# Cross attention's keys and values moved from their own stage into the core of the causal attention

## The reference: what is computed

```
x = x + memory_cross_attention(rmsnorm_2(x, norm_xa_w), rmsnorm_2(mem, norm_mem_w), wq, wkv, wo)

def memory_cross_attention(h, m, wq, wkv, wo):
    q = (h @ wq).reshape(b, s, XA_HEADS, XA_HEAD_DIM)
    k, v = jnp.split(m @ wkv, 2, axis=-1)
    scores = einsum('bshd,bmhd->bhsm', q, k) * XA_HEAD_DIM ** -0.5
    o = einsum('bhsm,bmhd->bshd', softmax(scores), v)
    return o @ wo
```

## Time and profile before

| | us |
|---|---|
| median of 3 runs | 2833.64 |
| lowest and highest | 2833.48, 2842.4 |
| the profiled execution's own time | 2844.55 |
| its span, from the first to the last instruction | 2842.8 |
| mean granted clock of PE | 0.949 |
| PE, DVE, POOL, ACT busy, share of the span | 84%, 57%, 52%, 24% |

### The profile page before, as it was taken

How to read it: one execution, slowest core, us unless ns; L and a number is a source line. 1 busy time by engine, 2 the same in 40 slices (tenths; PEclk the granted TensorE clock), 3 DMA queues, 4 the chain that set the end, 5 groups by cost and what they waited for, 6 DMA issues and landing times. The chain is left out here.

```text
span 2842.8 us, 28049 instructions
## 1 busy us (share of the span) xinstructions
PE 2389.1 (84%) x9104; PEld 1549.9 (55%) x9104; DVE 1634.2 (57%) x3467; ACT 690.4 (24%) x1777; POOL 1476.5 (52%) x962
## 2 busy tenths in 40 slices
PE   7999679998989988889886888888877777777776
PEld 6888567786878848767564344444322322222222
DVE  1266695224532648640228788888778777555555
ACT  2111234123421230222322222222222222111112
POOL 6777345673267712276365565666544444333432
PEclk9999789999899978889998999999999999999999
DMA  3222001221022200022226999999999999999996
GB/s 130 96 96 96 1 1 52 89 87 48 32 77 94 96 8 1 8 80 98 74 96 277 419 421 421 420 413 411 419 422 421 422 421 421 422 421 422 421 422 265
DMA packets 103878, 642.63 MB, mean 226 GB/s; under 512 B 12624, under 2 KB 13008, under 8 KB 38096
## 3 DMA queue, kind: packets, MB, share of 16 engines
q0 software_dynamic: 73728, 536.90, 45.5%
q1 hardware_dynamic: 30032, 104.24, 11.0%
HBM read 639.00 MB, written 2.10 MB: 226 GB/s over the span
## 5 line engine op out<-in xcount | busy, mean ns | idle before, releaser
L3041 PE MATMUL bank<-peer_row,peer_diag 128*128 128x512 f32 x2048 | 961.5, 615 | 284.8 <-ACT peer_diag L3020 283.8
L2963 POOL DMA_INDIRECT peer_row<-in_peer_uv,peer_ids x512 | 581.4, 1136 | 658.0 <-PE bank L3041 612.8
L3041 PEld LDWEIGHTS bank<-peer_row,peer_diag 128*128 128x128 f32 x2048 | 377.2, 193 | 838.3 <-ACT peer_diag L3020 451.6
L2986 DVE CUSTOM_DVE_ANT_0 peer_row<-peer_row,peer_h_tok 128x1024 f32<-128x1024 f32 x512 | 639.1, 1252 | 326.7 <-DMA peer_row<-in_peer_uv,peer_ids 326.6
L206 POOL TENSOR_TENSOR w_parts<-ring,zero 128x1024 fp32r<-128x1024 f32 x152 | 288.1, 1895 | 291.6 <-PE bank L283 129.4
L209 POOL TENSOR_TENSOR w_parts<-ring,w_parts 128x1024 fp32r<-128x1024 f32 x152 | 368.6, 2425 | 27.1 <-POOL w_parts L206 27.1
L3020 ACT ACTIVATE peer_diag<-ident,peer_weight 128x128 f32<-128x128 f32 x512 | 177.5, 394 | 241.5 <-DVE peer_weight L2978 241.5
L3024 ACT ACTIVATE peer_acts<-peer_dots 128x2 f32<-128x2 f32 x256 | 52.2, 204 | 743.3 <-DVE peer_dots L2986 743.3
L259 PE MATMUL bank<-ssm_h_high,w_parts 128*128 128x512 f32 x512 | 158.0, 389 | 0.8 <-DVEq L642 0.8
L259 PEld LDWEIGHTS bank<-ssm_h_high,w_parts 128*128 128x128 f32 x512 | 96.1, 188 | 21.0 <-DVEq L642 1.0
L2738 PE MATMUL bank<-peer_h_high,w_parts 128*128 128x512 f32 x256 | 107.4, 469 | 0.0
(11 more groups left out here) (542 smaller groups left out, 3841.8 us busy)
## 6 DMA issues: line engine op xcount, KB each, us to landing
ring<-in_weights SPq DMA_DIRECT2D x180, 512.0 KB, 3.3
peer_row<-in_peer_uv,peer_ids POOLq DMA_INDIRECT x512, 24.3
resid<-in_x SPq DMA_DIRECT2D x1, 2048.0 KB, 7.5
out<-resid SPq DMA_DIRECT2D x4, 512.0 KB, 7.6
xa_mem<-in_mem SPq DMA_DIRECT2D x1, 1024.0 KB, 4.9
peer_gain<-in_rows SPq DMA_DIRECT2D x2, 512.0 KB, 6.7
peer_keys<-in_peer_keys SPq DMA_DIRECT2D x1, 1024.0 KB, 7.3
ssm_o_gain<-in_rows SPq DMA_DIRECT2D x1, 512.0 KB, 3.4
```

The costliest lines, as they stand in the source:

```text
L2963: pool.indirect_dma_start(self.rows[row][:, :], None, self.m.ins["peer_uv"], bass.IndirectOffsetOnAxis(ap=self.choice.ids[:, t, slot:slot ...
L2986: dot = dve.tensor_tensor_reduce(mine, mine, self.tokens(slot_of(j)[0]), 1.0, 0.0, ALU.mult, ALU.add, self.dots[:, h % 4, r:r + 1])
L3041: mm = pe.matmul(self.m.banks[2 * t + half][:, :], self.diag[:, j % (2 * GROUP), :], self.rows[row][:, D + half * 512:D + (half + 1) * 512 ...
```

## The change

The normalised memory and the products with the weights of keys and values leave `hybrid_out_cross_in`:

- `mamba_out_attention_in` now also loads and normalises the memory. ACT issues the load after the norm that it has just made, waits for it, and then goes on; DVE sums squares and makes the diagonals ahead of the rotary angles; PE transposes the memory in two halves between units of the last chunk of the projection.
- `attention_core` gets 16 weight units: 8 for the values and 8 for the keys, both by `column`. One column stands before the first unit's turn, the others at the end of each unit. They share bank 7, so all of the attention's values go to bank 6, and values(u) waits for DVE's unit u-1. ACT copies each column out. The values come out with channels in the partitions; after units 4, 5, 8 and 9 PE turns four tiles of them (float32 transposes) and ACT copies these too. POOL splits the 16 units itself, both parts. SP stores values and keys (1 MB each) to a tensor in DRAM, and waits for the stores before the block's barrier.
- `hybrid_out_cross_in` is left with the mixer's output and the queries. At the end of its weight stream SP loads values and keys from DRAM and waits for them before the barrier. `high_weight` and `low_weights` are gone.
- In DRAM the weight units of keys and values stand behind the attention's input weights.

```diff
 def attention_core(...):
+        side = m.banks[7]
+        turn_after = {4: (0, 0), 5: (0, 1), 8: (1, 0), 9: (1, 1)}
+        copies_before = lambda u: u + sum(n < u for n in turn_after)
...
         @block.sync
             sp.dma_start(sinks[:, :], m.row("att_sinks", QH)).then_inc(sink_loaded, 16)
+            stream_weights(m, sp, N)
+            sp.wait_ge(side_copied, copies_before(max(turn_after)) + 2)
+            sp.dma_start(m.kept[0], mem_v[...]).then_inc(side_stored, 16)
+            sp.wait_ge(side_copied, N + len(turn_after))
+            sp.dma_start(m.kept[1], mem_k[...]).then_inc(side_stored, 16)
+            sp.wait_ge(side_stored, 32)
...
         @block.gpsimd
+            split_weights(m, pool, N)
...
         @block.tensor
             def values(u):
-                if u >= 2:
-                    pe.wait_ge(out_ready, u - 1)
+                if u >= 1:
+                    pe.wait_ge(out_ready, u)
...
+            def side_column(u):
+                pe.wait_ge(m.w_split, u_side + u + 1)
+                if u >= 1:
+                    pe.wait_ge(side_copied, copies_before(u))
+                column(m, pe, u, mem_h, side[:, 0:MEM]).then_inc(m.w_used, 1)
...
             scores(0)
             scores(1)
+            side_column(0)
             for u in range(N):
                 turn(u)
                 if u + 2 < N:
                     scores(u + 2)
+                if u in turn_after:
+                    side_turn(u)
                 if u >= 1:
                     values(u - 1)
+                if u + 1 < N:
+                    side_column(u + 1)
             values(N - 1)
...
         @block.scalar
                 if u >= 1:
                     turned_copy(u - 1)
+                act.wait_ge(m.w_used, u_side + u + 1)
+                to = values_ch[:, u, :] if u < DT else mem_k[:, u - DT, :]
+                act.activation(to, side[:, 0:MEM], ACT.Copy).then_inc(side_copied, 1)
...
 def hybrid_out_cross_in(...):
         @block.sync
-            sp.dma_start(mem[:, :, :], ins["mem"].rearrange("(t p) d -> p t d", p=P)).then_inc(mem_loaded, 16)
-            stream_weights(m, sp, 2 * DT + 2 * DT)
+            stream_weights(m, sp, 2 * DT)
+            sp.dma_start(v_tok[...], m.kept[0]).then_inc(kept_loaded, 16)
+            sp.dma_start(k_ch[...], m.kept[1]).then_inc(kept_loaded, 16)
+            sp.wait_ge(kept_loaded, 32)
...
         @block.tensor
-                if ch == 0 and kk == 2:
-                    norm_m.tensor(pe)
...
-            columns_out(m, pe, DT, mem_h, MEM, k_copied, 1, m.banks[4:8])
-            pe.wait_ge(q_copied, DT)
-            tokens_out(m, pe, 2, DT, mem_h, MT, v_done, nothing, lambda ch, t: m.banks[MT * ch + t])
```

More of the change, by code:

```diff
@@ L120, in __init__ @@
         self.floor = nc.sbuf_base
+        self.kept = nc.dram_tensor("xa_kept", [2, P, MT * D], F32, kind="Internal").ap()
     def sem(self, scope, name):
@@ L215, in split_weights @@
         four(i, u0, False)
[L218 to L232, removed]
 PASSES = ((0, 0), (0, 1), (1, 0))
@@ L1200, in before_bank, with memory, scalar @@
                 pe.wait_ge(self.read, TT * (ch - 2) + t + 1)
-        tokens_out(self.m, pe, self.CH, DT, self.h, TT, self.done, before_bank, self.bank_of, self.h_ready)
-    def scalar(self, act):
+        def memory(ch, kk):
+            if ch == self.CH - 1 and kk in (1, 2):
+                pe.wait_ge(self.read, TT * (self.CH - 1))
+                norm_m.tensor(pe, range(4 * kk - 4, 4 * kk))
+        tokens_out(self.m, pe, self.CH, DT, self.h, TT, self.done, before_bank, self.bank_of, self.h_ready, memory)
+    def scalar(self, act, norm_m):
         qk, v, gate = self.qk, self.v, self.gate
@@ L1340, in values @@
                     for half in halves:
-                        mm = pe.matmul(m.banks[6 + u % 2][:, q * AD:(q + 1) * AD],
+                        mm = pe.matmul(m.banks[6][:, q * AD:(q + 1) * AD],
                                        pt[:, u % 2, q, half * P:(half + 1) * P],
@@ L1345, in values, with side_turn @@
                 mm.then_inc(pv_done, 1)
+            def side_column(u):
[3 more added lines that the diff above has]
+                column(m, pe, u, mem_h, side[:, 0:MEM]).then_inc(m.w_used, 1)
+            def side_turn(u):
+                half, t = turn_after[u]
+                pe.wait_ge(side_copied, copies_before(u) + 1)
+                for k in range(4):
+                    mm = pe.transpose(side[:, k * P:(k + 1) * P], values_ch[:, 4 * half + k, t * P:(t + 1) * P], m.ident[:, :])
+                mm.then_inc(side_turned, 1)
             for j in range(NT):
@@ L2352, in _ @@
             turn.tensor(pe)
-            def beside(ch, kk):
-                if ch == 0 and kk == 2:
-                    norm_m.tensor(pe)
-            def before_bank(ch, t):
-                if ch == 1 and t == 0:
-                    pe.wait_ge(norm_m.turned_ready, DT)
-            out.tensor(pe, before_bank, beside)
+            out.tensor(pe)
             for k in range(DT):
@@ L3142, in program @@
         set_up(m)
-        qk, v, gate = mamba(m)
-        attention(m, qk, v, gate)
+        mem_h = [m.at(8 + 8 * x, f"xa_mem_h_{y}", [P, DT, MEM], F32R) for x, y in enumerate(("high", "low"))]
+        qk, v, gate = mamba(m, mem_h)
+        attention(m, qk, v, gate, mem_h)
         q_ch, k_ch, v_tok, rms = hybrid(m, qk, gate)
```

96 lines of the change are left out of this document (47 added, 49 removed).

## The result

| | before | after |
|---|---|---|
| median (us) | 2833.95 (5 runs) | 2818.65 (5 runs) |
| lowest and highest | 2833.48, 2842.4 | 2814.88, 2819.56 |
| the profiled execution's own time | 2844.55 | 2814.88 |
| its span | 2842.8 | 2813.2 |

The ratio is 0.9935, with a 95% interval of 0.9919 to 0.9951: 15.3 us faster, where 27 were forecast. The time lies in the stretched range of 2799 to 2823, but 5.7 us above the forecast's own, 2800 to 2813. Between the two profiled executions, by which the sum was made, the difference is 29.7, against -27.3 in the sum (and -29.6 by the two spans). So two questions remain: whether each term holds, and where the other 12 to 14 us are.

What follows compares the result with a forecast made beforehand. Outside PEER's gathers, PE's work, idle time and half clock were taken to set the core and tail. Terms -58.1 + 0 + 27.3 + 1 - 1 + 1.5 + 2 = -27.3 gave 2807 us at the median; own range 2800 to 2813, stretched 2799 to 2823.

Steps and rivals of the forecast that it cites:

- Rival 1: Causal core: the clock falls as it does now, 18 us at half clock costing 9 instead of 2: 2814; chance 0.19.
- Rival 3: Core: DVE and POOL stand in each other's way; if all waited, 11 us more, 2818; chance 0.06.
- Rival 4: Stored tensors late: store 9 us more, loads up to 29 more; with a third of that 2820; chance 0.09.
- The tail, -58.1: Block ahead of the cross core: without key and value work the cross core starts at 1326.9 instead of 1385.04, -58.1 us.
- the transposes, 0: Memory's transposes leave one PE-bound block, -3.7 us, and enter another, +3.7: zero in sum.
- ACT's delay in the projection: Projection block: ACT waits for the memory, some 12 us, hidden by 16.99 us of idle time; bounds 0 to +3.
- The core, +27.3 + 1 + 2 = 30.3: Causal core: columns +27.3 us, keys' store at its end +1, short clock falls in its first units +2.
- No falls at all: Core: by the skill's clock rule, columns in every gap would prevent clock falls, a time about 2 us lower.
- The start of the cross core, +1.5: Cross core: PE's pause before it brings half clock in its 16 first matmuls, +1.5 of at most +3.7 us.
- The -1 for the transposes behind the core: Next block's first 32 transposes (5.81 us at half clock) could take 3.7 if PE stays busy: -1 of -2.1 us.
- Rivals 2: Half clock through most of the core; at three quarters of the core 2880 us; chance 0.08.
- the difference is carried over to the median: Whole kernel: the profiled execution's 10.9 us above the median was taken off 2817.3, giving 2806.3.

Runs made afterwards that it cites:

- early: Changed kernel with the loads of stored values and keys issued ahead of the weight stream instead of behind it: 2813.52 us, ratio 0.9926.
- slim: Changed kernel with POOL splitting the first four units whole and only 16 of 1024 columns of the other twelve, all 24 matmuls kept: 2818.07 us, ratio 0.9931.
- thin: Changed kernel with one matmul a column instead of 24; loads, splits, waits and copies kept: 2799.92 us, ratio 0.9883.
- first repetition: Kernel before, unchanged, profiled again the first time: profiled execution 2834.35 us, core 76.94 us.
- a_again: Changed kernel run and profiled once more, nothing edited: median 2817.29 us, ratio 0.9928.
- b_again: Kernel before, unchanged, the first of its three repeated profiles: profiled execution 2834.35 us; median of all repetitions 2834.1 us.
- The filled gaps: Changed kernel without columns in the core, plus 50 matmuls nobody reads before and behind the first turns: median 2781.9 us, 2780.66 in the second profile.

## Why the prediction came out as it did

The direction, the mechanism and, to about 1 us each, the terms made from rows of the first profile were right; the step to the median was wrong. The median's place in the range of 2799 to 2823 is luck: it is above the forecast's own 2800 to 2813, and what stretched the range to 2823, rivals 1, 3 and 4, did not come.

- **The tail, -58.1, and the transposes, 0.** By the block lengths the tail lost 61.9 with the transposes in it and their new block won 4.1: -57.8 in all. The loads ended last, as said. PE's pause is 3.63 us, 4.3 were in the sum (1322.6 to 1326.9); from start to start, the cross core begins 4.02 us behind the last query matmul, where 4 to 5 were given. Rival 4's third of late transfers did not come; the keys' store landed in 3.9 us and was hidden, so its +1 was 0.
- **ACT's delay in the projection** was hidden: PE's only visible change there is the transposes, 2 x 1.95 = 3.9 us, and ACT still idles for 10.40 us ahead of chunk 1, where the earlier trace rows have 16.99.
- **The core, +27.3 + 1 + 2 = 30.3** (columns, store, clock dips) against 30.4 measured in the first pair of profiles. That the two agree to 0.1 is in part luck, since the store's +1 was 0: up to DVE's last instruction the core grew from 82.8 to 113.0 us, 30.2 where 29.3 were given. The unit was 6.79 for 6.75. The clock fell twice, in the opening transposes (6.22 us for 4.56) and under the last values (2.66 for 1.90), 2.4 us for the 2 given. No falls at all, the prediction's other possibility, came true where columns stand and not at the core's two ends.
- **The start of the cross core, +1.5** was +1.7, and early shows it to be the pause's price. The -1 for the transposes behind the core was hardly there: 5.58 us against 5.81.
- **Rival 1** had the stretches of 694 to 718 right and their owner wrong. The falls are not what the change keeps, but what only the old core has, in changing amounts. **Rivals 2 and 3** did not come: no window of the steady core is under 1.00, and slim shows that POOL's splits in twelve of the units cost nothing. **Rival 3** names a real effect, though, which thin brings out once PE no longer covers it.
- **The step that failed**: "the difference is carried over to the median", by which 2817.3 became 2806.3, with 2818.65 measured. It took the 10.9 us between the profiled execution and the median as common to both kernels. The first repetition's span is 10.2 shorter than that profile's, 6.8 of it in the core itself (76.94 against 83.76), 2.2 ahead of the Mamba output and 1.2 behind the core. So some 7 us lay in the very stretch that the change rebuilds and fills, and the full core, at 1.00 in its steady part in each of its profiles, has no such fall to lose or to save. Against the typical core the columns cost 114.14 - 76.94 = 37.2, not 30.4; with the tail (162.68 us in that repetition too) and the projection block that makes -61.9 + 4.3 + 37.2 = -20.4 against the first repetition; the whole difference from that one to the profile after is 2814.88 - 2834.35 = -19.5. The medians, -15.3 and -17.8 in the two comparisons, are smaller by a few us, and the profile after was itself the fastest of its five. The other pair of profiles near the medians, a_again against b_again, has -61.7 + 4.1 + 38.0 = -19.6 in the three blocks and +4.6 in stretches that the change leaves alone (1.9 ahead of the Mamba output, 1.7 behind the core, 1.1 from the cross core on), -15.0 in all. That is the medians' difference. What lengthens those stretches stays open: some of it moves from execution to execution, but in the stretch between the core and the block ahead of the cross core the four profiles of the kernel before have 459.25 to 460.47 us, and the two of the changed kernel and early's 460.95 to 461.75.

## What to carry to other kernels

Before a sum is made against a profiled execution, ask how far it lies from the median and in which stretch: if it is the stretch to be changed, its surplus belongs to the old code alone and does not carry over. Work that is put into gaps of a stretch with a shifting clock should be priced from the full length of that stretch in its usual state: here 46 us of matmuls went into a core of 77 us and cost 36 to 39. Loads that hold nobody up can be queued ahead of the weight stream; behind it they were the last wait of their block.

## What the runs showed of the hardware that was not expected

- The core before has the same instructions in 74.9, 76.9, 77.0 and 83.8 us, by a mean granted clock of 0.95, 0.89, 0.89 and 0.82, and 32 matmuls of 64 columns took 3.68 us in one execution and 6.93 in another at the same place in the program.
- The Trainium skill, "TensorE: Matmul & The Clock Gate", Part 1, has activity release the throttle. The filled gaps bear it out (0.51 becomes 1.00), and so do 12 matmuls a column: the clock stood at 1.00 from 680 to 770, with PE busy for 8.33 us of the 10 from 710 to 720.
- DVE's two-operand instruction from SBUF is held until POOL's instruction ends and 0.27 to 0.29 us more, in all eleven cases in thin. Where the gate started 0.01 us ahead of the split (719.29), the split was the one that took longer, 2.17 us in place of 1.89. In the changed kernel a gate met a split in the first three units only, for 2.12, 0.44 and 0.45 us, and from then on POOL waits for PE's column and the gate falls into that idle time. Take the column's work away and POOL runs nearly without a break; then ten in 16 take 1.28 us or more.
